# A hybrid decoder trunk on one core: rotations moved to tile ends, convolution taps and norms spread over the attention's half steps

## The reference

```python
proj = h @ w_in
aq, ak, av, dq, dk, dv, db, da, dz, cv = jnp.split(proj, idx, axis=-1)
q = partial_rope(aq...); k = partial_rope(ak...)       # 8 query heads, 2 key heads of 64
y_attn = swa_attention(q, k, v, sinks)                 # window of 128, in 4 blocks of 128 queries
qkv = silu(causal_dwconv(concat([dq, dk, dv]), dn_conv_w))
o = gated_delta_rule(l2norm(dq), l2norm(dk), dv, g, beta)   # 4 heads, 8 chunks of 64 tokens
o = o * rsqrt(mean(o * o) + EPS) * dn_norm_g * silu(dz)
u = causal_dwconv(ca * sigmoid(cb), cv_dw_w) + cv_dw_b      # 31 taps on 256 channels
y_cv = silu(layernorm(u, cv_ln_g, cv_ln_b))
return concat([y_attn, y_dn, y_cv]) @ w_out
```

## Time and profile before

| what | value |
|---|---|
| median of 3 runs | 1717.74 us |
| profiled execution, its own time | 1719.74 us |
| its span (first to last instruction) | 1717.6 us |
| PE busy | 1577.8 us (92%) |
| DVE busy | 1176.6 us (69%) |
| ACT busy | 816.7 us (48%) |
| granted TensorE clock, mean | 0.939 of full |

### The profile page before, as it was taken

How to read it: one execution, slowest core, us unless ns; L and a number is a source line. 1 busy time by engine, 2 the same in 40 slices (tenths; PEclk the granted TensorE clock), 3 DMA queues, 4 the chain that set the end, 5 groups by cost and what they waited for, 6 DMA issues and landing times.

```text
span 1717.6 us, 22333 instructions
## 1 busy us (share of the span) xinstructions
PE 1577.8 (92%) x8916; PEld 1237.3 (72%) x8916; DVE 1176.6 (69%) x1376; ACT 816.7 (48%) x948; POOL 58.4 (3%) x49
## 2 busy tenths in 40 slices
PE   6999978997999998998999888979999999999993
PEld 5667755776888886886677656748888888888883
DVE  4676785485666664444647764358888888888884
ACT  2453225423232221113552254257777777777775
POOL 6300000000000000000000000020000000000001
PEclk9899987897999998998999987989999999999996
DMA  8262220062555554441211200459999999999974
GB/s 322 98 220 87 75 99 1 12 243 89 184 183 174 185 181 134 163 145 49 62 52 49 61 3 1 153 205 375 401 387 396 384 392 392 390 387 386 395 276 159
DMA packets 93575, 341.37 MB, mean 199 GB/s; under 512 B 9888, under 2 KB 13984, under 8 KB 90784
## 3 DMA queue, kind: packets, MB, share of 16 engines
q1 hardware_dynamic: 91168, 331.56, 53.1%
q0 software_dynamic: 2304, 8.39, 1.3%
HBM read 317.89 MB, written 22.02 MB: 198 GB/s over the span
## 4 chain that ended last, share of the span: by engine, by line
PE 85%; DVE 8%; ACT 4%; issue 2%; DMA 1%; SPq 0%; POOL 0%; DVEq 0%; ACTq 0%; POOLq 0%
PE ps L601 35%; PE ps L1123 10%; PE ps L1121 10%; PE ps L1122 10%; DVE scr L1571 3%; PE ps L587 2%; DVE scr L1568 2%; PE ps L573 1%; PE ps L930 1%; PE ps L904 1%; PE ps L580 1%; PE ps L756 1%; PE ps L614 1%; PE ps L615 1%; PE ps L916 1%
## 5 line engine op out<-in xcount | busy, mean ns | idle before, releaser
L1164 ACT ACTIVATE whi<-raw 128x1024 fp32r<-128x1024 f32 (+1 forms) x114 | 125.5, 1103 | 393.0 <-PE ps L601 369.7
L601 PE MATMUL ps<-hhi,whi 128*128 128x512 f32 x720 | 300.7, 418 | 2.4 <-ACT sg L1433 2.4
L1568 DVE TENSOR_TENSOR wlm<-rawm,hlo 128x2048 fp32r<-128x2048 f32 x120 | 274.7, 2290 | 36.3 <-ACT hlo L1215 34.6
L601 PE MATMUL ps<-hhi,wlo 128*128 128x512 f32 x720 | 288.6, 401 | 0.0
L601 PE MATMUL ps<-hlo,whi 128*128 128x512 f32 x720 | 287.6, 399 | 0.0
L1215 ACT ACTIVATE hlo<-rawm 128x2048 fp32r<-128x2048 f32 x120 | 230.1, 1918 | 79.1 <-PE ps L1123 78.7
L1578 DVE TENSOR_TENSOR wlo<-raw,whi 128x1024 fp32r<-128x1024 f32 (+1 forms) x114 | 147.4, 1293 | 169.5 <-ACT whi L1164 167.7
L1122 PE MATMUL ps<-wlm,xgh 128*128 128x512 f32 x480 | 187.7, 391 | 0.0
L601 PEld LDWEIGHTS ps<-hhi,whi 128*128 128x128 f32 x720 | 137.5, 191 | 48.4 <-issue 14.2
L601 PEld LDWEIGHTS ps<-hlo,whi 128*128 128x128 f32 x720 | 137.6, 191 | 34.1 <-issue 3.9
L601 PEld LDWEIGHTS ps<-hhi,wlo 128*128 128x128 f32 x720 | 137.2, 191 | 32.9
(11 more groups left out here) (309 smaller groups left out, 2461.7 us busy)
## 6 DMA issues: line engine op xcount, KB each, us to landing
rawm<-in_wm SPq DMA_DIRECT2D x360, 512.0 KB, 7.6
raw<-in_w SPq DMA_DIRECT2D x98, 512.0 KB, 3.5
adah<-in_ada SPq DMA_DIRECT2D x56, 512.0 KB, 4.4
scr<-in_ada SPq DMA_DIRECT2D x20, 1024.0 KB, 6.5
raw<-in_w SPq DMA_DIRECT2D x16, 704.0 KB, 4.3
xs<-scr SPq DMA_DIRECT2D x15, 512.0 KB, 5.5
ys<-yb SPq DMA_DIRECT2D x15, 512.0 KB, 8.8
xg<-xs SPq DMA_DIRECT2D x14, 512.0 KB, 7.4
```

Source lines behind the costliest of these rows:

```text
L601: ins = pe.matmul(ps[:, b, :], a, r[:, k0 + k, :], start=(start and first and k == ks[0] and n == 0), stop=(stop and last and k == ks[-1] ...
L1164: act.activation(whi[:, slot, 0:width], raw[:, slot, 0:width], ACT.Copy).then_inc(sem("hi_ready"), 1)
L1568: return dve.tensor_tensor(out, a, b, op)
```

## The change

Nothing is computed differently; work is placed elsewhere and two copies change engine.

- Tiles: the copy of the turned values goes from DVE (t = 12) to ACT (t = 11, behind that tile's own copy). The copy of the solve's result is one ACT copy of 128 x 2048. Each `rotate(c)` goes from the middle of tile 12 + c to its end, behind `inverse_y` or `scan_step` there. On DVE `roped` stands one t later (13 to 17). The low parts of tiles 18 and 19 are split behind state updates.
- Taps: the first side is six taps ahead of the second. Tile 9 gets six; the half steps 0 to 4 and 6 get two each (the last gets what is left, one), in place of six in each of half steps 0 and 1.
- Half steps: `scan_step(4)` stands ahead of the loop and `(5)`, `(6)` in half steps 1 and 2; `outputs` in 4 (was 6), `output_sums` in 6 (was 9), the convolution's sums in 9 and 11 (were 1 and 3). ACT's and DVE's parts follow. ACT issues one more `exps` ahead of its long passes in half steps 7, 11 and 13.

The core of the diff:

```diff
                 for c in range(5):
-                    middle.setdefault(12 + c, []).append(lambda c=c: rotate((4, 0, 1, 2, 3)[c]))
-                middle[16].append(lambda: scan_step(0))
-                after[16] = [lambda: scan_step(1)]
+                    after.setdefault(12 + c, []).append(lambda c=c: rotate((4, 0, 1, 2, 3)[c]))
+                middle[16] = [lambda: scan_step(0)]
+                after[16].insert(0, lambda: scan_step(1))
...
+                scan_step(4)
                 for i in range(STEPS):
...
-                    if i in (0, 2, 4):
-                        scan_step(4 + i // 2)
-                    if i == 1:
+                    if i in (1, 2):
+                        scan_step(4 + i)
+                    if i == 4:
+                        outputs()
+                    if i == 6:
+                        output_sums()
+                    if i == 9:
+                        pe.wait_ge(sem("orms_ready"), v)
                         conv_sum(CY, "taps_done", "cmean_done")
-                    if i == 3:
+                    if i == 11:
                         conv_sum(UT, "csq_ready", "cvar_done")
...
-                    if i == 6:
-                        pe.wait_ge(sem("crms_ready"), v)
-                        outputs()
-                    if i == 9:
-                        output_sums()
...
+                def values_by_token():
+
+                    act.wait_ge(sem("vt_done"), v)
+                    act.activation(VTOK, ps[:, 6, :].rearrange("p (n d) -> p n d", n=4), ACT.Copy)\
+                        .then_inc(sem("vtok_ready"), 1)
...
-                    if i + 1 < STEPS:
-                        exps(i + 1)
+                    ahead = i + (3 if i in (7, 11, 13) else 2)
+                    while begun < min(i + 2, STEPS):
+                        exps(begun)
+                        begun += 1
                     turned(i)
+                    while begun < min(ahead, STEPS):
+                        exps(begun)
+                        begun += 1
...
+                    if i == 7:
+                        act.wait_ge(sem("oss_done"), v)
+                        mark(act.activation(ORMS, ps[:, 6:8, :]..., ACT.Ln, ...), "act_step")
+                        act.activation(ORMS, ORMS, ACT.Exp, scale=-0.5).then_inc(sem("orms_ready"), 1)
...
-                    if lv > 1:
-                        taps(3)
+                    taps((6, 4, 4, 4, 3)[lv - 1])
...
-                    if 12 <= t < 17:
-                        roped((4, 0, 1, 2, 3)[t - 12])
+                    if t >= 13:
+                        roped((4, 0, 1, 2, 3)[t - 13])
...
-                    if i < 2:
-                        taps(6 if i == 0 else 2 * CV_K)
...
+                    if i == 5:
                         dve.wait_ge(sem("o_chunks"), 8 * v)
...
+                    if i < 7 and i != 5:
+                        taps(2)
...
+                    if i == 9:
                         dve.wait_ge(sem("orms_ready"), v)
                         tt(YD, YD, ORMS).then_inc(sem("yd_ready"), 1)
+                    if i == 10:
+                        dve.wait_ge(sem("cmean_done"), v)
...
+                    if i == 13:
+                        dve.wait_ge(sem("crms_ready"), v)
```

More of the change, by code:

```diff
@@ L1395, in _ @@
                             .then_inc(sem("yhi_ready"), 1)
[L1396 to L1408, removed]
+                    if i == 14:
+                        attended(2)
                 attended(3)
@@ L1768, in roped @@
                     mark(tt(q, q, ROTT, ALU.add), "roped")
-                tap_list = [(d, n) for d in range(CV_K) for n in range(2)]
+                lead = 6
+                tap_list = [(d, 0) for d in range(lead)]
+                for d in range(CV_K):
+                    tap_list += [(d, 1)] + ([(d + lead, 0)] if d + lead < CV_K else [])
                 def taps(m):
@@ L1825, in _ @@
                         keys_scaled()
-                    split(T_IN[layer] + t + 2)
+                    if t < 16:
+                        split(T_IN[layer] + t + 2)
                     if t == 1:
@@ L1847, in _ @@
                         ada_groups((G_IN + (2 if t == 6 else 3),))
[L1848 to L1853, removed]
-                        queries_less_absorbed()
-                        taps(2)
+                    if 10 <= t < 15:
+                        taps((3, 3, 3, 4, 6)[t - 10])
+                    if t == 15:
+                        taps(2)
+                        queries_less_absorbed()
+                        taps(3)
+                    if t == 16:
+                        state(0)
+                        taps(3)
+                        state(1)
+                        split(T_IN[layer] + 18)
                     if t == 17:
-                        taps(2)
+                        state(2)
+                        taps(3)
+                        split(T_IN[layer] + 19)
+                        state(3)
                 def maxima(i):
@@ L1899, in _ @@
                     maxima(i)
-                    if i < 2:
-                        taps(6 if i == 0 else 2 * CV_K)
[L1902 to L1910, removed]
+                    if i in (1, 2, 3):
+                        state(3 + i)
                     if i in (6, 10, 14):
                         normed(i // 4 - 1)
[L1913 to L1916, removed]
                     if i in (8, 12):
                         attended(i // 4 - 2)
-                    if i == 9:
-                        dve.wait_ge(sem("yhi_ready"), 6 * layer + 2)
-                        tt(hlo[:, 6:8, :], cy, hhi[:, 6:8, :].bitcast(F32), ALU.subtract).then_inc(sem("ylo_ready"), 1)
+                    if i == 5:
                         dve.wait_ge(sem("o_chunks"), 8 * v)
@@ L1927, in _ @@
                              "o_read")
[L1928 removed]
+                    if i < 7 and i != 5:
+                        taps(2)
+                    if i == 7:
+                        taps(2 * CV_K)
+                        for n in range(2):
+                            dve.wait_ge(sem(f"tap{n}"), CV_K * v)
+                        dve.sem_inc(sem("taps_done"), 1)
+                    if i == 9:
                         dve.wait_ge(sem("orms_ready"), v)
                         tt(YD, YD, ORMS).then_inc(sem("yd_ready"), 1)
+                    if i == 10:
+                        dve.wait_ge(sem("cmean_done"), v)
+                        mark(stt(cy, ps[:, 6:7, :].broadcast_to([P, 2, S]), -1.0 / 256, cy), "cxc_ready")
+                    if i == 11:
+                        dve.wait_ge(sem("yhi_ready"), 6 * layer + 2)
+                        tt(hlo[:, 4:6, :], YD.rearrange("p (a s) -> p a s", a=2), hhi[:, 4:6, :].bitcast(F32), ALU.subtract)\
+                            .then_inc(sem("ylo_ready"), 1)
+                    if i == 13:
+                        dve.wait_ge(sem("crms_ready"), v)
+                        dve.wait_ge(sem("csq_ready"), v)
+                        tt(cy, cy, rstd[:].unsqueeze(1).broadcast_to([P, 2, S])).then_inc(sem("cn_ready"), 1)
                     if i == 15:
                         dve.wait_ge(sem("yhi_ready"), 6 * layer + 4)
[L1933 to L1934 removed]
+                        tt(hlo[:, 6:8, :], cy, hhi[:, 6:8, :].bitcast(F32), ALU.subtract).then_inc(sem("ylo_ready"), 1)
                 attended(2)
```

37 lines of the change are left out of this document (18 added, 19 removed).

## The result

The kernel after takes 1761.51 us (median of 4 runs, 1759.64 to 1763.35) beside 1716.8 us for the kernel before on the same chip: ratio 1.0266, 95% interval 1.0247 to 1.0286. It is slower. The forecast was 1748 us in a range of 1717 to 1772. The profiled execution took 1759.64 us with a span of 1757.3, which is 39.7 more than before; the granted clock fell from 0.939 to 0.929. Times and ratios are of fast executions; one of `e_start_without_taps` took 4645 us and is left out.

The account below looks back on a forecast made before the run. PE was taken to bound the kernel, with 85% of the chain of waits. Tiles +26.7 and half steps +3.4 gave +30.1 on the profiled 1719.74, 1749.8 us; that execution lay 2.0 above the median, so 1748, range 1717 to 1772.

Parts of the forecast that it names:

- Rotation waits at tile ends: Behind tiles 13 to 15 PE waits for DVE's ropes; with a scan step 13.9 us a layer, 27.8 in both.
- The clock behind them: Low clock behind the six new rotation pauses: 2.4 us each, 14.4 in all; bounds nothing and 7.8 us each.
- rival 3: Clock stays at 1.2 GHz from tile 14 to 17, +27 us a layer: 1775 us, or 1801 in both; chance 0.11.
- What goes in the tiles: Old waits for values' copy, rotated keys, third query tile and state go: 12.7 us, plus 5.1 of clock.
- The tile term: Tiles of both layers: new waits, taps and clock less the old waits and their clock, +26.7 us.
- The half steps' later pauses: After `outputs`, attends in half steps 5 to 13 wait 3.5, 5.6 and 5.7 us for DVE, a last one 3.7 for ACT.
- The start of the half steps: First scores to the end of `outputs`: 22.4 us, pauses of at most 1.4 us, no charge for the clock.
- rival 1: Clock forgives small pauses, half steps keep 2.4 GHz (-14.6 us), tile pauses cost no clock (+12.3): 1715 us; chance 0.13.
- half-step term: Half steps of both layers: 87.1 and 85.2 us against 88.1 and 80.8, +3.4 us.
- Behind the last half step: After the last attend, layer 0's modulation sums add 1.9 us, making 78.1 us against layer 1's 76.2 before clock.
- Early exponentials worth little: Extra `exps` ahead of ACT's long passes gain little, because the attends and DVE are late, not `exps`.
- Table loads by the trace: ACT's table change in the half steps costs its 1.28 us load, without the skill page's drain of about 1.38.

Follow-up runs that it names:

- e_start_without_taps: Kernel after, with the eleven taps of half steps 0 to 4 and 6 all issued in half step 7; ratio 1.0268 to the kernel before.
- e_filled_pauses: Kernel after, with 18 matmuls whose result nobody reads ahead of each of the three late rotations of a layer; ratio 1.0211 to the kernel before.
- e_middle_norms_first: Kernel after, rotations and ropes back in their old places, DVE's three products that wait for ACT one half step later, behind `normed`; ratio 0.9977 to the kernel before.
- e_rotations_middle: Kernel after, with rotations back in the middle of tiles 12 to 16 and ropes at t = 12 to 16; ratio 1.0137 to the kernel before.
- e_middle_old_half_steps: Kernel before, with only both copies on ACT, the spread taps and the splits of tiles 18 and 19 behind state updates; ratio 0.9921 to the kernel before.

## Why the prediction was right, and which terms were off

- **Rotation waits at tile ends: right.** Predicted 4.6, 4.5 and 4.5 a layer and 27.8 in all with a scan step; measured 4.72, 4.61 and 4.61, 27.9 in all, plus 0.9 for the scan steps. Reading DVE's queue as it stood in the earlier trace rows, and asking what PE has left to do meanwhile, gave the length to 0.1 us.
- **The clock behind them: right.** Predicted 14.4, measured 13.5 to 16.3 (e_filled_pauses). The bound of 7.8 each, rival 3, did not come: the clock was back at 1.00 between the pauses.
- **What goes in the tiles: as predicted,** all of the 4.7 for the values' copy; `inverse_x` waits 1.9 us in all instead of 1.2, where I had added 2.3, too much. The tile term as a whole is +24.8 by the cuts (27.6 with the other executions' layer 0), forecast +26.7.
- **The half steps' later pauses: the order right, the sizes nearly.** Attends predicted late by 3.5, 5.6 and 5.7, measured 3.85, 6.16 and 5.83. The last one, on ACT, was 1.47 and not 3.7. From the end of `outputs` to the end of the last attend I had 53.8 + 9 of clock = 62.8 us; it was 61.2 (278.3 to 339.6).
- **The start of the half steps: this term was mis-sized.** I wrote "I get the end of `outputs` 22.4 us after the first scores, with pauses of at most 1.4 us", and gave this stretch no charge for the clock. The pauses were as short as I said, at most 0.6 us at the scores, but the stretch took 28.0 us, and the clock stood at 1.2 GHz for 23.9 us of it, from 253.2 on. No run here takes this low clock away, so that it makes the difference is read from the trace and not tested. The row that should have warned me was my own: in 256.5 to 272.2 of the kernel before PE was busy and slow, in this very stage. The prediction gives no reason for leaving it out; rival 1 only has the long pause ahead of it going, and the low clock did not go with the pause (27.3 and 17.1 us of it before, 23.9 in each layer after). That is 5.6 us a layer, 11.2 in all, of a half-step term that came to +12.7 against +3.4.
- **Behind the last half step,** layer 0's modulation sums took 3.2 us instead of the 1.9 that I had (the clock was at 1.2 GHz there too, from 338.5 on), and the rest of the program is 2.2 us longer.
- **Early exponentials worth little: right** (1.0247 without them).
- **Table loads by the trace: right.** ACT's load starts at 298.34 and its pass at 299.63, 0.01 us behind the load's end, so no drain is there to be added.

```profile
298.34 1.28 ACT L1400 ACT_TABLE_LOAD   x1
299.63 1.11 ACT L1400 ACTIVATE scr<-ps,cst 128x1024 f32<-128x1024 f32 x1
```

Rival 1, in which the clock forgives, would have needed high clocks in the half steps; they were 0.70 and 0.71. The sum was +30.1 and the span grew by 39.7; the missing 9.6 is the start (11.2) and the sums and the rest (about 3.5), less what I had charged too much in the tiles and behind `outputs` (about 5).

## What to carry to other kernels

Behind a producer and its consumer on two engines there must be other work on the waiting engine: the same five DVE operations behind tile 13 cost no wait with half a tile of matmuls and the solve ahead of the rotation, and 4.7 us, plus 2.3 to 2.7 of clock, without them. An instruction that waits for a third engine should stand behind what the bottleneck waits for; moving three such products one place down was worth 1.6% of this kernel. And when a long pause is removed, do not assume that the slow clock behind it goes too: look at what the clock does in the stage as a whole.

## What the runs showed of the hardware that was not expected

- **PE can be almost fully busy at 1.2 GHz for long.** After, it was busy for 16.48 of 17.0 us at 0.50, with no wait over 0.6 us since the rotation at 231.3. In e_middle_norms_first it was busy for 36.4 of 37.5 us at 1.2 GHz, with one wait of 1.0 us; in e_rotations_middle for 33.8 of 37.5, with a wait of 2.45 us near the end. All these stretches began 3 to 5 us behind the first scores. There, in the kernel after, PE was busy for 75 and 84% of two stretches:

```profile
250.30:252.80 2.50, 1.87 (x20) 1.34 (x16) 2.07 (x5) 2.10 (x3) 0.00 (x0) 1.00 0.04 10
252.80:255.30 2.50, 2.11 (x14) 1.52 (x14) 2.40 (x6) 0.88 (x4) 0.00 (x0) 0.58 0.91 239
```

  What in it lowers the clock is open: neither the taps on DVE nor the tile pauses are the cause, since the stretch was there without the one (e_start_without_taps) and without the other (e_rotations_middle, e_filled_pauses). Its length goes with the new order of the half steps: e_middle_old_half_steps and e_rotations_middle differ in the half steps alone, and have 10.2 and 37.5 us at 1.2 GHz there. Which of the moved pieces does it was not tried.
- **The same wait is worth different times.** The low clock behind a pause of 4.6 us cost 2.7 us in layer 1's tiles and 1.8 to 2.7 in layer 0's. In the half steps each pause of 3.85 to 6.16 us came with 6.8 to 10.2 us at 1.2 GHz, from within the pause or its end on, where the eight matmuls of an attend took 1.81 to 1.94 us instead of 1.00.
- **Useless matmuls in a pause hold the clock,** at 1.00 through the tiles, and moved the whole kernel from 1.0266 to 1.0211.
